# Down weights of the last four experts in eight transfers, by column and contraction halves

## The reference

```python
hid = silu(einsum('sd,edf->sef', xs, w_gate)) * einsum('sd,edf->sef', xs, w_up)
moe = einsum('sef,efd->sd', hid * cs[..., None], w_down)     # 32 experts, f = 256, d = 1024
h = h + moe
h_next = h * rsqrt(mean(h * h, axis=-1) + EPS) * gain        # next layer's norm, or the final one
```

## Time and profile before

| | |
|---|---|
| median of three runs | 727.35 us |
| profiled execution, its own time | 729.75 us |
| its span, first to last instruction | 728.0 us |
| PE busy | 620.7 us (85%) |
| DVE busy | 301.0 us (41%) |
| ACT busy | 242.6 us (33%) |
| DMA | 244.52 MB, mean 336 GB/s |
| mean granted TensorE clock | 0.941 |

### The profile page before, as it was taken

One profiled execution on the slowest core, in us unless ns is written; L12 is line 12 of the kernel. 1 busy time (PEld: TensorE's weight loads), 2 busy tenths in 40 slices (PEclk: granted clock), 3 DMA queues, 4 the chain that ended last, 5 costly groups with the idle time before them and its releaser, 6 DMA issues.

```text
span 728.0 us, 11030 instructions
## 1 busy us (share of the span) xinstructions
PE 620.7 (85%) x4456; PEld 408.3 (56%) x4456; DVE 301.0 (41%) x518; ACT 242.6 (33%) x540; POOL 35.4 (5%) x64
## 2 busy tenths in 40 slices
PE   9998899999998595675989999999999966595685
PEld 7997787786542341323269987887754431341321
DVE  4556787533232211312285698652522330220304
ACT  5525555451211110100157685662511110110112
POOL 3020000000000100000000001060000000000000
PEclk9999999999999897978999999999999998797979
DMA  8969137798999999999996636569999999999993
GB/s 315 240 234 317 75 116 267 284 407 326 393 422 400 405 422 421 420 423 421 408 387 240 228 123 228 172 266 403 398 386 391 415 422 421 421 422 420 423 415 138
DMA packets 59712, 244.52 MB, mean 336 GB/s; under 512 B 4545, under 2 KB 8913, under 8 KB 38930
## 3 DMA queue, kind: packets, MB, share of 16 engines
q1 hardware_dynamic: 58400, 242.33, 85.0%
q0 software_dynamic: 768, 1.40, 1.0%
q10 hardware_dynamic: 498, 0.15, 0.2%
HBM read 242.82 MB, written 1.05 MB: 335 GB/s over the span
## 4 chain that ended last, share of the span: by engine, by line
PE 51%; DMA 33%; SPq 6%; DVE 5%; issue 2%; ACT 2%; DVEq 0%; ACTq 0%
DMA ring<-in_moe_w_down 31%; PE psum L2279 7%; PE psum L1850 6%; PE psum L2224 6%; PE psum L1861 3%; PE psum L1854 3%; SPq L541 3%; PE psum L2217 3%; PE psum L1859 3%; PE psum L1852 3%; DMA ring<-in_att_w_in 3%; PE psum L2359 2%; SPq L508 2%; PE psum L2361 2%; PE psum L2360 2%
## 5 line engine op out<-in xcount | busy, mean ns | idle before, releaser
L2224 PE MATMUL psum<-arena,xT 128*32 128x512 f32 x512 | 66.0, 674 | 34.5 <-DMA arena<-in_moe_w_up 34.5
L1567 DVE TENSOR_TENSOR arena<-psum,arena 128x256 f32<-128x256 f32 x16 | 6.8, 424 | 212.2 <-ACT arena L1051 212.2
L2224 PE MATMUL psum<-ring,xT 128*32 128x512 f32 x512 | 64.6, 659 | 34.7 <-DMA ring<-in_moe_w_up 34.7
L1047 ACT ACTIVATE arena<-psum 128x256 f32<-128x256 f32 x16 | 6.1, 383 | 203.0 <-PE psum L2224 203.0
L2279 PE MATMUL psum<-ring,arena 128*32 128x512 f32 x456 | 60.3, 612 | 13.5 <-DMA ring<-in_moe_w_down 13.5
L2217 PE MATMUL psum<-arena,xg 128*128 128x128 f32 x512 | 62.4, 280 | 0.8 <-DVE arena L1553 0.8
L2217 PEld LDWEIGHTS psum<-arena,xg 128*128 128x128 f32 x512 | 60.3, 196 | 2.7 <-issue 2.7
L2224 PEld LDWEIGHTS psum<-arena,xT 128*32 128x32 f32 x512 | 17.2, 122 | 78.5 <-issue 43.0
L2224 PEld LDWEIGHTS psum<-ring,xT 128*32 128x32 f32 x512 | 16.5, 120 | 75.4 <-issue 39.3
L1850 PE MATMUL psum<-x_hi,w_hi 128*128 128x256 f32 x224 | 56.0, 288 | 2.2 <-DVE x_hi L1252 1.2
L2208 PE MATMUL psum<-xT,arena 128*128 128x512 f32 x128 | 57.7, 594 | 0.0
(11 more groups left out here) (341 smaller groups left out, 1044.7 us busy)
## 6 DMA issues: line engine op xcount, KB each, us to landing
ring<-in_moe_w_down SPq DMA_DIRECT2D x54, 1024.0 KB, 20.6
ring<-in_moe_w_gate SPq DMA_DIRECT2D x32, 1024.0 KB, 15.7
ring<-in_moe_w_up SPq DMA_DIRECT2D x32, 1024.0 KB, 17.6
arena<-in_moe_w_gate SPq DMA_DIRECT2D x32, 1024.0 KB, 21.3
arena<-in_moe_w_up SPq DMA_DIRECT2D x32, 1024.0 KB, 23.1
ring<-in_rec_w_in SPq DMA_DIRECT2D x16, 1024.0 KB, 13.9
ring<-in_att_w_in SPq DMA_DIRECT2D x8, 1024.0 KB, 11.4
ring<-in_att_w_out SPq DMA_DIRECT2D x4, 1024.0 KB, 16.6
```

The source lines that it names most:

```text
L2224: return pe.matmul(bank(3)[e * CAP:(e + 1) * CAP, :].rearrange("p (w f) -> p w f", w=2), gatheredT[:, k, e * CAP:(e + 1) * CAP], w, start= ...
```

## The change

The last quad's down weights come in eight transfers of 512 KB instead of four of 1 MB: column half 0 with both contraction halves first, then column half 1 with its two. Each piece is 2 KB instead of 4 KB; a transfer has 256 pieces as before. The four parts (column half c, contraction half j) report to three semaphores; one of these was `cmp_w1_rest` and is now called `rest_loaded`. On PE, `down` for the last quad becomes `last_down`, called four times, and `combine` of the last quad is done in two halves: half 0 stands ahead of the part (1, 1), half 1 behind it. The programs of DVE and ACT are as before.

```diff
+LAST_PARTS = ((0, 0, "last_down_front"), (0, 1, "last_down_front"), (1, 0, "rest_loaded"), (1, 1, "last_down_back"))
...
             v = moe_w_down[l].rearrange("(q e) (p j) n -> q j p e n", e=QE, p=P)[NQ - 1]
-            for j in range(KF):
+            for c, j, done in LAST_PARTS:
                 for i, slot in enumerate(down_slots(l, True)):
-                    sp.dma_start(slot.rearrange("p (e j n) -> p e j n", e=2, j=KF)[:, :, j, :],
-                                 v[j][:, 2 * i:2 * i + 2, :])\
-                        .then_inc(s["last_down_back" if j else "last_down_front"], 16)
+                    sp.dma_start(slot.rearrange("p (e j n) -> p e j n", e=2, j=KF)[:, :, j, c * 512:(c + 1) * 512],
+                                 v[j][:, 2 * i:2 * i + 2, c * 512:(c + 1) * 512]).then_inc(s[done], 16)
...
-            def combine(l, m, gathers=None):
+            def combine(l, m, gathers=None, halves=(0, 1)):
...
                     half, t = divmod(i, 2)
+                    if half not in halves:
+                        continue
...
-            def down(l, n, last_quad=False, early=False):
+            def last_down(l, c, j):
+
+                part = LAST_PARTS[2 * c + j][2]
+                pe.wait_ge(s[part], 32 * (l + 2) if c and not j else 32 * (l + 1) * (2 - c))
+                for e in range(QE):
+                    last = pe.matmul(bank(5 + c)[e * CAP:(e + 1) * CAP, :], hidT[:, j, e * CAP:(e + 1) * CAP],
+                                     down_part(l, NQ - 1, e, j)[:, c * 512:(c + 1) * 512],
+                                     start=(j == 0), stop=(j == KF - 1))
+                if j == KF - 1:
+                    last.then_inc(s[f"down{l}" if c else f"down_front{l}"], 1)
+
+            def down(l, n, early=False):
...
                 pe.wait_ge(s[f"added{l}"], 4 * end)
                 combine(l, end - 1)
-                down(l, end, last_quad=True)
+                pe.wait_ge(s[f"hidT{l}"], end + 1)
+                last_down(l, 0, 0)
+                last_down(l, 0, 1)
+                last_down(l, 1, 0)
                 pe.wait_ge(s[f"added{l}"], 4 * end + 4)
-                combine(l, end)
+                combine(l, end, halves=(0,))
+                last_down(l, 1, 1)
+                combine(l, end, halves=(1,))
```

More of the change, by code:

```diff
@@ L448, in load @@
             for i, (part, src) in enumerate(parts):
-                sp.dma_start(part(dst), src).then_inc(arrived if i < 2 else s["cmp_w1_rest"], 16)
+                sp.dma_start(part(dst), src).then_inc(arrived if i < 2 else s["rest_loaded"], 16)
         def load_ring(sp, u, parts):
@@ L1950, in _ @@
             w1 = unit(U_CMP).rearrange("p (w j n) -> p w j n", w=2, n=P)
-            pe.wait_ge(s["cmp_w1_rest"], 32)
+            pe.wait_ge(s["rest_loaded"], 32)
             pe.wait_ge(s["kv2_done"], 7)
@@ L2260, in turn_hidden @@
                 last.then_inc(s[f"hid_psum{l}"], 1)
-            def down(l, n, last_quad=False, early=False):
+            def last_down(l, c, j):
[8 more added lines that the diff above has]
+            def down(l, n, early=False):
                 pe.wait_ge(s[f"hidT{l}"], n + 1)
-                if last_quad:
-                    pe.wait_ge(s["last_down_front"], 32 * (l + 1))
-                elif early:
+                if early:
                     pe.wait_ge(s[f"down_loaded{l}"], 80 + 16 * n)
@@ L2272, in down @@
                     pe.wait_ge(s[f"down_loaded{l}"], 64 * n + 32)
-                kind = n if early else NQ - 1 if last_quad else 2
+                kind = n if early else 2
                 for j in range(KF):
-                    if last_quad and j:
-                        pe.wait_ge(s["last_down_back"], 32 * (l + 1))
                     for c in range(2):
```

## The result

22 runs of each kernel gave a median of 729.3 us after the change and 728.17 us before it. The ratio is 1.0016, with a 95% interval of 1.0009 to 1.0024: 1.2 us slower (0.7 to 1.75). The forecast was +1.35 us, laid upon the median of the first three runs, 727.35 us; so it is the difference that is compared here and not the 728.7 us. One of the 22 runs before took 2090.38 us, the others 726.28 to 729.45 us; without it the median is 728.02 us.

What follows compares the result with a forecast made beforehand. The DMA of down weights into the ring, 31% of the span, was taken to bound the kernel. +0.60 us in layer 0 and +0.74 in layer 1 gave +1.34, so 728.7 us; range 728.2 to 729.3, with rivals 727.3 to 729.9.

Steps and rivals of the forecast that it cites:

- The decisive step: On DVE, all four adds wait behind the copy of bank 6: first add 0.56 to 0.64 (layer 0), 0.70 to 0.78 us (layer 1) later.
- Two sums on PE: In the last quad, half of combine holds PE for 1.76 us ahead of the last block.
- The landing: Last down weights land at 363.7 and 715.8 by 387 GB/s, hidden behind combine with 0.9 to 1.3 us to spare.
- the rival of the late part: At 333 GB/s the last weights land 0.5 us past PE's need in each layer: +2.3 us, 729.7 us; chance 0.12.
- The rest of the chain: From the first add to the norm the length stays, since ACT's first three squares pace it.
- The rival of the adds ahead: DVE adds half 0 before its copy, so the norm comes 0.36 us earlier in all: 727.0 us; chance 0.07.

Runs made afterwards that it cites:

- Adds first: Changed kernel with DVE's two adds of column half 0 moved ahead of its copy of bank 6; ratio 1.0000 to the kernel before.
- blocks first: Changed kernel with PE doing all four blocks of the last quad, then the whole combine; run twice, ratios 1.0013 and 0.9988 to the kernel before.
- mean on DVE: Kernel before with one small step (L819, mean of the first half row) moved from ACT to DVE, between its adds; ratio 0.9993.
- loads alone: Kernel before with only the loads altered: eight 512 KB transfers in 2 KB pieces, contraction half 0 first; ratio 1.0015.
- mixed loads: Changed kernel with contraction half 0 in two 1 MB transfers, half 1 in four of 512 KB, all four blocks before combine; ratio 0.9985 to before.

## Why the prediction was right

**The decisive step held.** DVE's copy starts at T + 5.76 in both layers, and the first add right behind it at T + 6.37; the prediction had T + 5.62 and T + 6.23 to 6.31. Adds first shows that this order is needed for the loss: with the adds ahead of the copy, the same transfers and the same order on PE lose 0.05 us. It is not enough by itself: in blocks first DVE keeps this order, and with the last block no longer behind two sums the loss is gone too. PE's new order and DVE's old one make the loss together. The Trainium skill, Perfetto Trace Analysis, section Per-engine timelines, calls DVE a strict first-in, first-out engine; the trace agrees: DVE stood idle although two sums were finished 1.9 and 1.0 us before the copy (adds first takes them at T + 3.88 and 4.74).

**One term was mis-sized, by 0.14 us.** Two sums on PE were put at 1.76 us, half of 3.52. From the start of half a `combine` to the next block it is 1.90 (716.07 - 714.17). Some 0.08 us of this could have been read from the earlier trace rows: the `combine` without a wait, from which 3.52 was taken, is 3.60 us long there, and the one that starts behind a wait, as the half `combine` does, 3.68. The other 0.06 us stays open; the semaphore wait ahead of block (1,1), which the prediction took at nothing, is one candidate. The half `combine` itself started where it should, at T + 2.73. The rest moved with it: the first add follows the copy's start after 0.61 us, the shorter of the prediction's two values, and the norm came 0.69 and 0.82 us later against T instead of 0.60 and 0.74. The profiles' sum is 1.51 us, and the interval of the measured 1.2 us (0.7 to 1.75) holds both it and the forecast. That forecast and measurement lie only 0.15 us apart is in part luck, since the interval is about 1 us wide.

**The landing was right, and hidden.** The last part lands at T + 3.2 in layer 0 and about T + 3.0 in layer 1; the prediction's 387 GB/s gave T + 3.1 and 3.2. With PE coming at T + 4.63, 1.4 us and more are to spare, so the rival of the late part fell. (The prediction's times for the parts before it, 713.5 and 710.8, are those of 374 GB/s; by 387 they are 713.1 and 710.4, and PE waited for neither.) The 341 GB/s of the Trainium skill, DMA: Bandwidth & Descriptors, section Bandwidth, were measured with transfers issued from GpSimd. By them the landing is estimated at T + 4.6 to 4.7; in SP's full queue the trace shows it about 1.4 us and more ahead of that estimate.

**The rest of the chain kept its length.** From the first add to the norm it is 4.20 us (10.57 - 6.37) and was 4.21 (9.88 - 5.67), and mean on DVE confirms that ACT's squares set this pace. The rival of the adds ahead was right as a sum: it gave -0.36 us, and with the 0.14 us that each layer had been put too low -0.08; measured in the profiles, +0.05.

**What remains open.** Whether blocks first by itself is faster than the kernel before: its two ratios contradict each other in sign. And whether loads alone lost by the size of its pieces or by the number of its transfers: no run alters one without the other.

## What to carry to other kernels

Before work is moved ahead on one engine, follow it through the program of the next: here the sums were early, but the engine that takes them had a waiting copy in front. Splitting a transfer in order to start sooner gained here only where the last part ended PE's wait (blocks first and mixed loads, by the norm against T); on an engine that is busy anyway, work put ahead of the last part was work put into the path. Small fixed steps on the engine that sets the pace of a tail (0.33 us on ACT, twice) are worth looking for first.

## What the runs showed of the hardware

SP spent 24.9 and 24.6 us on the eight issues of a layer, against 11.3 and 15.4 on the four before. The issues of L542, all of 256 pieces, took between 0.39 and 9.84 us:

```profile
L542 SPq DMA_DIRECT2D ring<-in_moe_w_down x16: 385/1530/9840, 326.6 to 703.0; - x16
```

So the making of the pieces takes at most 0.39 us, and the rest is put down to waiting for room in the queue. It cost nothing that a trace shows, since the queue stayed full. Busy time of the changed kernel while the eight transfers land in layer 0 (DMA share 1.05, 386 GB/s):

```profile
352.00:361.00 9.00, 9.00 (x60) 3.04 (x52) 3.68 (x6) 1.86 (x4) 0.00 (x0) 1.00 1.05 386
```

Eight transfers in 2 KB pieces brought the last 4.19 MB 0.6 us later than four in 4 KB pieces (loads alone), in a queue that is always full; the prediction's two stretches of the profile before (387 against 403 GB/s) made it 0.4 us. The 387 GB/s were reached with 1 MB transfers in 2 KB pieces, the 386 with 512 KB transfers in such pieces. That speaks for the size of the pieces as the cause, and not the number of transfers.
